# Expert layers of a decoder trunk: 32 more tokens through gathered U rows, narrower U products, gates shared with ScalarE

## What is computed

```
q = (h @ w_q) per head, two halves of 128
s = q . keys  -> top 16 of 128 in each half -> top 16 of the 16 x 16 sums
idx = i * 128 + j ; gate = softmax over the 16 of a head
act = gelu(u_tab[idx] . h)              # 128 experts of each token
y   = sum over slots of gate * act * v_tab[idx]
x   = layer_norm(ALPHA * x + gate2 * y)
```

## Time and profile before

| | |
|---|---|
| median of the runs | 3312.33 us |
| profiled execution, first to last instruction (the page gives no other time of it) | 3305.3 us |
| TensorE busy | 3189.0 us, 96% |
| DVE busy | 2607.8 us, 79% |
| GpSimd busy | 2052.8 us, 62% |
| ScalarE busy | 1161.1 us, 35% |
| moved by DMA | 856.31 MB, 259 GB/s in the mean |
| mean granted TensorE clock | 0.988 |

### The profile page before, as it was taken

One profiled execution on the slowest core, in us unless ns is written; L12 is line 12 of the kernel. 1 busy time (PEld: TensorE's weight loads), 2 busy tenths in 40 slices (PEclk: granted clock), 3 DMA queues, 4 the chain that ended last, 5 costly groups with the idle time before them and its releaser, 6 DMA issues. The chain is left out here.

```text
span 3305.3 us, 57051 instructions
## 1 busy us (share of the span) xinstructions
PE 3189.0 (96%) x21428; PEld 2745.2 (83%) x21428; DVE 2607.8 (79%) x4810; ACT 1161.1 (35%) x1786; POOL 2052.8 (62%) x1304
## 2 busy tenths in 40 slices
PE   8998998899999999999999898999999999999998
PEld 3445887699999999888888777999999998888886
DVE  8583664589998886689899765899988866888997
ACT  0113544233334443333333423333344333333333
POOL 1122444377785655788888603777855568888884
PEclk9999998999999999999999999999999999999999
DMA  9750002377787887999999623777878889999995
GB/s 336 279 207 29 3 4 98 121 255 262 256 280 240 308 323 290 378 348 344 360 352 342 215 83 129 255 265 255 277 249 306 317 296 377 346 347 361 349 342 179
DMA packets 364075, 856.31 MB, mean 259 GB/s; under 512 B 32969, under 2 KB 201393, under 8 KB 355538
## 3 DMA queue, kind: packets, MB, share of 16 engines
q1 hardware_dynamic: 278610, 542.98, 47.3%
q0 software_dynamic: 85248, 310.42, 26.2%
HBM read 750.46 MB, written 102.81 MB: 258 GB/s over the span
## 5 line engine op out<-in xcount | busy, mean ns | idle before, releaser
L1804 PE MATMUL peer_acc<-peer_hhi,peer_uhi 128*128 128x384 f32 x2048 | 697.1, 340 | 8.4 <-POOL peer1same_ulo L2004 4.5
L1804 PE MATMUL peer_acc<-peer_hlo,peer_uhi 128*128 128x384 f32 x2048 | 686.2, 335 | 0.0
L2004 POOL TENSOR_TENSOR peer1same_ulo<-peer_u,peer_uhi 128x1024 fp32r<-128x1024 f32 x128 | 311.7, 2438 | 192.1 <-ACT peer_uhi L1884 190.7
L2004 POOL TENSOR_TENSOR peer0same_ulo<-peer_u,peer_uhi 128x1024 fp32r<-128x1024 f32 x128 | 311.7, 2438 | 191.9 <-ACT peer_uhi L1884 191.1
L1880 ACT ACTIVATE peer_gel<-peer_acc 128x384 f32<-128x384 f32 x256 | 125.7, 491 | 768.9 <-PE peer_acc L1804 768.9
L1804 PEld LDWEIGHTS peer_acc<-peer_hhi,peer_uhi 128*128 128x128 f32 x2048 | 386.3, 189 | 11.4 <-POOL peer1same_ulo L2004 5.8
L1804 PEld LDWEIGHTS peer_acc<-peer_hlo,peer_uhi 128*128 128x128 f32 x2048 | 386.2, 189 | 1.0 <-issue 0.5
L2035 POOL TENSOR_TENSOR peer0lsame_vlo<-peer0l_v,peer0l_vhi 128x1024 fp32r<-128x1024 f32 x128 | 310.3, 2424 | 85.6 <-ACT peer0l_vhi L1919 85.2
L2035 POOL TENSOR_TENSOR peer1lsame_vlo<-peer1l_v,peer1l_vhi 128x1024 fp32r<-128x1024 f32 x128 | 310.2, 2424 | 85.4 <-ACT peer1l_vhi L1919 84.7
L2067 DVE SCALAR_TENSOR_TENSOR peer_acc<-peer_row,peer_p_g,peer_acc 128x1024 f32<-128x1024 f32 x254 | 325.1, 1280 | 36.1 <-DMA peer_row<-in_pe_v,peer_idx 36.1
L1804 PE MATMUL peer_acc<-peer_hhi,peer0same_ulo 128*128 128x384 f32 x1024 | 343.7, 336 | 0.0
(11 more groups left out here) (453 smaller groups left out, 6892.7 us busy)
## 6 DMA issues: line engine op xcount, KB each, us to landing
peer_u<-in_pe_uT SPq DMA_DIRECT2D x256, 512.0 KB, 5.8
peer0l_v<-in_pe_v SPq DMA_DIRECT2D x128, 512.0 KB, 6.0
peer1l_v<-in_pe_v SPq DMA_DIRECT2D x128, 512.0 KB, 6.1
activations<-peer_gel SPq DMA_DIRECT2D x256, 192.0 KB, 6.1
rw_g<-in_ada POOLq DMA_DIRECT2D x60, 512.0 KB, 5.4
routing<-peer0m_wb SPq DMA_DIRECT2D x24, 1024.0 KB, 8.3
peer0l_wt<-routing SPq DMA_DIRECT2D x64, 384.0 KB, 7.5
peer0l_gl<-activations SPq DMA_DIRECT2D x128, 192.0 KB, 7.1
```

The costliest lines, as they stand in the source:

```text
L1804: mm = pe.matmul(ub[e % 2][:, 0:SD], a, h[:, k, 0:SD], start=(n == 0), stop=(n == 3 * KT - 1))
L2004: g.tensor_tensor(ulo[:, q].rearrange("p k e -> p (k e)"), u[:, q].rearrange("p k e -> p (k e)"), uhi[:, e % NH].bitcast(F32).rearrange("p ...
```

## The change

The last 32 tokens of the third dense tile (tokens 352 to 383, `OWN`) get their activations from gathered U rows as well. The 128 partitions hold four copies of these 32 tokens (`COPIES`), each with a quarter of the slots, so 32 further gathers and dots do (`idx_own`, `dots_own`, and `h_own`, an SBUF tile with four copies of their h). The indices are moved to the copies by SyncE after each head, the dots back to the 32 tokens' partitions by SyncE in the blocks; gelu, the product with the gate and a turn by TensorE put gate x activation into `slotT` in place of the gate, ahead of the groups of these tokens. So their routing holds activation x gate, and their activations in the V phase are ones. The U products, the gelu, its store and its load are 352 wide (`UD`). For both one-hots DVE makes one comparison of 2 x 4 x 128 (`pair`); three of four gate products go to ScalarE (`gate_group`), one stays on DVE. The ring has 7 rows, and the dots are spread differently.

```diff
-NG = 8
+NG, OWN, COPIES = 7, 32, 4
-HEAD_DOTS = 10
+HEAD_DOTS = 8
+LAST_DOTS = 16
-EARLY_ROWS = 16
+EARLY_ROWS = 8
+ACT_GATES = 3
+MOVE_AT, OWN_GELU_AT, OWN_TURN_AT, DOTS_END = 14, 16, 20, 8
...
+        UD = SD - OWN
+        DOTS = SLOTS + OWN_SLOTS                   # 160
+        IN_BLOCKS = DOTS - LAST_DOTS - AT_DOTS     # 85 (57 before)
 dots_by:
-            return min(AT_DOTS + (SLOTS - AT_DOTS) * (e - AT_BLOCKS) // (DT * BLOCK_TILES), SLOTS)
+            if e < AT_LAST:
+                return AT_DOTS + IN_BLOCKS * (e - AT_BLOCKS) // (DT * BLOCK_TILES)
+            return min(DOTS - LAST_DOTS + 3 * (e - AT_LAST), DOTS)
+        def dot_of(m):          # from dot 8 to 71 every other one is of the 32 tokens
 rows_by, rows_after:
-            return min(max(0, 2 * (e - AT_LAST - 1)), EARLY_ROWS)
+            return min(max(0, 2 * (e - AT_LAST - DOTS_END - 1)), EARLY_ROWS)
-            return min(EARLY_ROWS + 14 * (e + 1) // 15, SLOTS)
+            return min(EARLY_ROWS + e + 1, SLOTS)
 SyncE:
+                for c in range(COPIES):
+                    sp.dma_start(h_own[copies[c]], x_sb[own, OT]).then_inc(h_copied, 16)
...
+                    if r == 2 and 1 <= n <= HEADS:
+                        move_idx(n - 1)         # waits for idx_made, then four small copies
+                    if e == AT_BLOCKS + MOVE_AT:
+                        sp.wait_ge(dot_done, MIXED)
+                        ...                     # four copies dots_own -> dots_turned
 TensorE:
-                            mm = pe.matmul(ub[e % 2][:, 0:SD], a, h[:, k, 0:SD], ...)
+                            mm = pe.matmul(ub[e % 2][:, 0:UD], a, h[:, k, 0:UD], ...)
 spread_group:
+                    pe.wait_ge(gated, ACT_GATES * (n + 1))
-                    pe.wait_ge(j_made, n + 1)
 ScalarE, after the copies of the tile's groups, for the next tile's groups:
+                def gate_group(n):
+                    act.wait_ge(j_made, n + 1)
+                    if n >= 2:
+                        act.wait_ge(spread_done, n - 1)
+                    if n * G == UD:
+                        act.wait_ge(own_taken, 1)
+                    for q in range(ACT_GATES):
+                        a.activation(hot_i[:, n % 2, q], pair[n % 2][:, 0, q], ACT.Copy,
+                                     scale=slotT[:, 0, n * G + q:n * G + q + 1]).then_inc(gated, 1)
-                    if e == AT_LAST:
-                        act.wait_ge(dot_done, SLOTS)
+                    if e == AT_LAST + DOTS_END:
+                        act.wait_ge(dot_done, DOTS)
 GpSimd:
+                    if mine:
+                        pool.wait_ge(idx_moved, 16 * COPIES * (s // HEAD_OWN + 1))
-                    if e >= AT_LAST + FETCH_LAG:
+                    if e >= AT_LAST + DOTS_END + FETCH_LAG:
 DVE, at the layer's start:
+                dve.wait_ge(h_copied, 16 * COPIES)
+                ch(v.scalar_tensor_tensor(out=h_own[:], in0=h_rows[1][:], scalar=1.0, in1=h_own[:], op0=ALU.add, op1=ALU.mult))
+                ch(v.tensor_tensor(h_own[:], h_own[:], h_rows[0][:], ALU.add))
 dot:
+                    v.scalar_tensor_tensor(out=row[:, m % NG], in0=row[:, m % NG], scalar=1.0, in1=h_own[:] if mine else h_g, ...)
 groups:
-                    v.tensor_tensor(hot_j[n % 2], iota_p ... [P, G, P], spread(slotT[:, 2, n * G:(n + 1) * G], P), ALU.is_equal)
-                    for q in range(n * G, (n + 1) * G):
+                    v.tensor_tensor(pair[n % 2], iota_p ... [P, 2, G, P], slotT[:, 1:3, n * G:(n + 1) * G] ..., ALU.is_equal)
+                    for q in range(n * G + ACT_GATES, (n + 1) * G):
 before the V phase:
+                dve.wait_ge(w_stored[1], 16 * PIECES * DT)
+                ch(v.memset(gl[:, :, UD:SD], 1.0))
```

More of the change, by code:

```diff
@@ L1576, in phase_peer @@
         assert LAST_TILES >= NU + HALF_TILES and GROUPS % BLOCK_TILES == 0
+        UD = SD - OWN
+        OT, OWN_SLOTS, HEAD_OWN = DT - 1, SLOTS // COPIES, TOPK // COPIES
+        DOTS = SLOTS + OWN_SLOTS
+        MIXED = FIRST_DOTS + 2 * OWN_SLOTS
+        own = slice(P - OWN, P)
+        copies = [slice(OWN * c, OWN * (c + 1)) for c in range(COPIES)]
         AT_DOTS = FIRST_DOTS + (HEADS - 2) * HEAD_DOTS + BETWEEN_DOTS
+        IN_BLOCKS = DOTS - LAST_DOTS - AT_DOTS
         V_TURNS = (ET - NU - 2) // TURN
@@ L1732, in _ @@
                         load_head(n + 2)
+                    if r == 2 and 1 <= n <= HEADS:
+                        move_idx(n - 1)
+                    if e == AT_BLOCKS + MOVE_AT:
+                        sp.wait_ge(dot_done, MIXED)
+                        to = dots_turned[own].rearrange("t (n c i) -> t n c i", c=COPIES, i=HEAD_OWN)
+                        for c in range(COPIES):
+                            sp.dma_start(to[:, :, c], dots_own[copies[c]].rearrange("t (n i) -> t n i", i=HEAD_OWN)).then_inc(dots_moved, 16)
                     hh, r = divmod(e - AT_BLOCKS, HALF_TILES)
@@ L1829, in _ @@
                             mm.then_inc(slots_turned, 1)
+                    if e == AT_BLOCKS + OWN_TURN_AT:
+                        pe.wait_ge(own_made, 1)
+                        pe.matmul(four[2][:, 0:OWN], dots_turned[own], const["ident"][own, own], start=True, stop=True).then_inc(own_turned, 1)
                     u_product(e)
@@ L1946, in _ @@
                     tile_step(e)
+                    if e == AT_BLOCKS - TURN_AT + 1:
+                        act.wait_ge(slotT_made, 3)
+                        gate_group(0)
+                        gate_group(1)
+                    if e == AT_BLOCKS + OWN_GELU_AT:
+                        act.wait_ge(dots_moved, 16 * COPIES)
+                        a.activation(dots_turned[own], dots_turned[own], ACT.Gelu).then_inc(own_gelu, 1)
+                    if e == AT_BLOCKS + OWN_TURN_AT:
+                        act.wait_ge(own_turned, 1)
+                        a.activation(slotT[:, 0, UD:SD], four[2][:, 0:OWN], ACT.Copy).then_inc(own_taken, 1)
                     if n < HEADS and r == 0:
@@ L2131, in _ @@
                 dve.wait_ge(slots_made, 1)
-                ch(v.tensor_copy(gate_g[:], slots[:, 0, GT]))
+                ch.send(v.tensor_copy(gate_g[:], slots[:, 0, GT]))
+                ch(v.tensor_copy(p_g[own], slots[own, 0, OT]))
                 may_dot[0] = AT_DOTS
@@ L2148, in _ @@
                     ins.then_inc(i_made, 1)
-                    may_dot[0] = AT_DOTS + (SLOTS - AT_DOTS) * (n + 1) // (DT * GROUPS)
+                    if n == A_TILE * (OWN_GELU_AT + 2):
+                        dve.wait_ge(own_gelu, 1)
+                        v.tensor_tensor(dots_turned[own], dots_turned[own], p_g[own], ALU.mult).then_inc(own_made, 1)
+                    may_dot[0] = AT_DOTS + IN_BLOCKS * (n + 1) // (DT * GROUPS)
                     while n_dots[0] < may_dot[0]:
                         fill()
+                for m in range(n_dots[0], DOTS):
+                    dot(m)
+                n_dots[0] = DOTS
                 dve.wait_ge(dots_gelu, 1)
```

98 lines of the change are left out of this document (64 added, 34 removed).

## The result

The changed kernel takes 3347.68 us (median of 4 runs, 3342.68 to 3363.3), the kernel before in the same session 3312.18 (3311.42 to 3317.51): a ratio of 1.0115, 95% interval 1.009 to 1.0139. It is 1.1% slower where 2.0% faster was forecast; the time is outside the range.

The account below looks back on a forecast made before the run. TensorE, busy 96% of the span, was taken to bind; -41.0 + 1.5 + 0 + 0.5 + 4.6 + 1 = -33.4 us a layer, -66.8 for two, gave span 3238.5, plus 7.0 rim: 3246 us, range 3229 to 3278.

Parts of the forecast that it names:

- +0.6 a dot: Heads: dots with two SBUF inputs stand during POOL's subtractions, 0.6 us each (bounds 0 and 2.1); DVE 40.8 a head, cost 0.
- rival 2: Heads: two-SBUF dots bind at 0.9 us extra each, a head needs 42.0, time 3262; chance 0.14.
- signs of being wrong: Blocks' tile stays at 5.9 us or more, TensorE waits for slots ahead of the blocks, or last tiles take 75 or more.
- The U product, -41 a layer: U tiles: 352 instead of 384 columns, 160.0 ns a product, 3.85 us a tile, 41.0 us less a layer.
- Blocks: Block tiles: 5.64 us instead of 5.96, DVE, ACT and POOL fitting; late rows cost 1.5 us a layer.
- rivals 1 and 3: Blocks: first, DMA engines bind, 3283, chance 0.12; third, gathered rows come too late in burst tiles, 3323, chance 0.04.
- rival 4: U products: time doesn't follow columns, the weight load binds at 173 ns, only additions stay, 3327; chance 0.02.
- ACT's gate product: Blocks: six gate products a tile on ACT at 0.3 us each (bounds 0.25 and 0.4), hidden with 0.6 to spare.
- Last U tiles, 10.6 of stand: Last 16 U tiles: TensorE stands 10.6 us against 6.0, from POOL's gathers and V start; +4.6 a layer (0 to 12).
- V and after, +1: V phase: 120 rows at one a tile, 1.43 MB a tile instead of 1.41; +1 us a layer (0 to 6).
- layer start, +0.5: Before head 0: four copies and two more DVE instructions of 1.2 us; cost 0.5 us a layer (0 to 2).
- The rim, 7.0: Whole kernel: the runs' median lies 7.0 us above the profiled execution's span, and this was kept in the forecast.

Follow-up runs that it names:

- e3: Changed kernel with the own tokens' dots reading h_g from PSUM instead of h_own from SBUF (wrong activations): 3265.42 us, ratio to before 0.9865.
- e6: Kernel before with only the narrower U products, and 8 instead of 10 dots per head: 3240.95 us, ratio 0.9795.
- e9: Changed kernel, complete, with the 32 own dots moved to the first 18 block tiles and reading PSUM, h_own swapped with h_g: 3265.65 us, ratio 0.9861.
- e10: As e9, with 9 instead of 8 dots per head and 10 instead of 16 in the last tiles: 3257.89 us, ratio 0.9842.
- e1: Kernel before with only U products, gelu stores and U loads 32 columns narrower, those tokens' activations left out: 3260.46 us, ratio 0.985.
- e11: As e10, with 12 instead of 8 V rows before the V stage and 29 rows in 30 V tiles: 3262.94 us, ratio 0.9852.
- e7: Changed kernel with even and odd swapped, so own dots come first among the heads' mixed dots: 3325.48 us, ratio 1.0051.

## Why the prediction was wrong

- **The step that failed: the heads, "+0.6 a dot", cost 0.** The mechanism was named (DVE stands while POOL subtracts) and rival 2 was built on it, but the price was taken from a random meeting: 53% of the time times a residual of 1.2. The two engines are not random to each other; their order repeats with each head, so the meeting repeats. Measured +1.24 a dot (bounds given: 0 to 2.1), and the lag pushed an old instruction, the candidates' sum, into the same place. The forecast had DVE at 40.8 us a head. In the head from 2319.47 to 2368.39 (48.9 us) its four own dots took 5.50, 2.31, 2.70 and 1.45, 4.7 more than forecast; the sum took 4.16 (+2.9); two other old instructions with two inputs in SBUF (L2191, L2200) took 2.1 more, and one (L2201) 2.1 less. That makes 48.4. So DVE was not level with TensorE's 40.8 but 8 us over it in such a head, and the stands that followed brought half clock.
- **What that cost.** The span came out 111.0 us over the forecast (3349.5 against 3238.5). 82.6 of it are in the heads and between, +41.6 where the 64 shorter tiles a layer should have given -41.0 in all; with the operand in PSUM (e3) 69.2 of these are gone. 22.0 are in the blocks and the last U tiles, of which 11.3 are gone in e3. 7.9 are in V and after; 1.5 are off ahead of the heads, in the kernel's favour.
- **Its own signs.** Two of the signs of being wrong came: TensorE waited 6.0 us for the slots in each layer, and the last tiles took over 75 us. The heads' period of 43.0 is in the earlier trace rows; the two rows give 42.4, over the first four heads.
- **Rival 2** (0.9 each, 3262) had the right engine and stopped at the dots; its range ended where the damage began.
- **The U product, -41 a layer.** Right in pitch: 3.84 to 3.87 a tile. Realised: 33 (e6). The heads gave 16.6 of 20.5, and the last U tiles 1 of 5.1: already full on DMA, they keep what their products save.
- **Blocks.** 5.64 a tile, DVE's comparison 1.22, no ceiling of DMA at 355 GB/s and 0.95: right, and rivals 1 and 3 did not happen; rival 4 neither. ACT's gate product took 0.39, the upper bound, and TensorE waited for it 8.0 us in all; cost forecast 0.
- **Last U tiles, 10.6 of stand.** They stood 11.1 and 12.3 (79.2 less 66.9 in layer 1), and TensorE was busy for 66.9, which is 5.3 over 16 x 3.85 (before the change it was 2.4 over), at a granted clock of 0.94. The stage took 78.4 and 79.2 where 74.6 was forecast. What bound was not POOL's issue order, as the working had it, but bytes: 30.2 MB at 381 GB/s. A single U tile took 23.55 us to land there:
```profile
2747.20 23.55 DMA peer_u<-in_pe_uT
```
  The window of before already showed 0.97 busy at 377 GB/s, 28.3 MB in 75.0 us; two more megabytes at that rate are 5 us, as much as the products save. The step counted issues and should have counted bytes.
- **V and after, +1; layer start, +0.5.** V and after came out +4.7 and +5.1. TensorE is busy in nearly all of V, but not at its very start: 4.2 us in layer 0 and 4.8 in layer 1 are lost over the first 48 of its 2304 products. In layer 1 an old instruction of DVE, the low part of the second weighed tile (two SBUF inputs; 0.55 us at the same place before), meets two subtractions of POOL:
```profile
2808.13 5.63 DVE L2257 TENSOR_TENSOR peer1l_plo<-kept_g_row,peer1l_phi 128x384 fp32r<-128x384 f32 x1
```
```profile
2808.63 4.70 POOL L2112 TENSOR_TENSOR peer1lsame_vlo<-peer1l_v,peer1l_vhi 128x1024 fp32r<-128x1024 f32 x2
```
```profile
2813.91 0.60 PE L1894 MATMUL peer_acc<-peer1l_vhi,peer1l_phi 128*128 128x512 f32 x1 [2.85 <-DVE peer1l_plo L2257]
```
  TensorE stands 2.85 us for it and then makes eight products at half clock. It is the same kind of collision as in the heads, and in layer 1 it is there in e3, e9 and e10 as well (5.62 to 5.64 us), whose own dots read PSUM; in e1 and e11 the instruction took 0.55. In layer 0 it took 0.55 too. There TensorE stood 2.23 us at the same product, after DVE had waited 3.7 us for activations to land; what holds these up was not followed. In e11 DVE waited 3.8, 2.5, 3.9 and 1.2 us for them in layer 1.
- **The rim, 7.0.** The profiled execution after took 3351.31 for a span of 3349.5: 1.8. The 7 came from setting one execution's span beside the median of others; 5.2 of them say that the profiled execution of before was a fast one, which changes nothing in the forecast.

## What to carry to other kernels

Before pricing an added instruction by an average of collisions, ask whether the two engines are locked to one beat; if they are, the price is that of its place, it repeats in every turn, and it can drag its neighbours along. An operand's place can be worth more than the operation: look at which inputs lie in SBUF and move the one that can go to PSUM, by a swap if PSUM is full. After any change of order, look at the old instructions as well: the new ones need not be those that pay. Where a stage shows its DMA engines at 0.97, price what is added in bytes.

## What the runs showed of the hardware

- A 128x1024 DVE instruction with two SBUF inputs takes 1.21 to 1.23 us alone, and up to 6.47 where two GpSimd subtractions follow each other; with one input in PSUM it took 1.19 to 1.22 in all 320 cases of e3.
- An instruction with a single SBUF input can be held too: the conversion of 128x128 positions took 0.22 us in the median before, 3.52 in e7 and 2.7 in e6, each of these beside subtractions.
- It works in the other direction as well: 57 of the 576 gathers that GpSimd issued in the changed kernel took about 1.76 us in place of 0.95 to 1.1 (46 of them beside a DVE instruction with two SBUF inputs), 10 of 512 before, one of 576 in e3 and none in e9.
- ScalarE's 128x128 copy with a scale from SBUF took 0.39 us where its gelu of that shape took 0.30.
- The DMA engines held 379 to 396 GB/s around the last U tiles in five kernels, at a share of 1.00 to 1.02, and 349 to 353 in the V stage at the same share (e9, e10, e11): the same full share moves different amounts in different stages.
